# Adding two groups of output projections ahead of queued weights, and summing a norm's squares from folded halves

## The chip, the cores and the metric

One core of a Trainium2 chip runs the whole program in one launch. The metric is the device time in microseconds (us); lower is better.

## What is computed

Two transformer blocks over 256 tokens of width 1024, all in float32. The first block is causal attention and a convolutional feed-forward, with a norm at its end; the second is feed-forward, a mixer of two kinds of attention, and feed-forward again, each with a norm whose gain and shift come from a conditioning vector. Cut to the parts that matter here:

```
x = x + attention(rms_norm(x)) @ w_o            # phases qkv1, o1
x = x + conv_ffn(rms_norm(x))                   # phases up1, down1
x = rms_norm(x)
x = x + gate1 * swiglu(modulate(rms_norm(x)))   # phases up2, down2
x = x + gate2 * mixer(modulate(rms_norm(x)))    # phases qkv3, o3
x = x + gate3 * swiglu(modulate(rms_norm(x)))   # phases up4, down4

rms_norm(x) = x * rsqrt(mean(x * x, over the 1024 features) + eps) * gain
```

## The kernel before

The activations stay on the chip, transposed: `XT` holds 8 tiles of 128 features by 256 tokens. Each product in a phase takes its weights as slabs of 8 (or 6) row tiles by 256 columns. A slab is loaded by DMA into `raw` (3 buffers), ScalarE (ACT) rounds it by pairs of row tiles (a chunk, 128x512) into `whi`, VectorE (DVE) takes the rest into `wlo`, and TensorE (PE) multiplies each row tile in three matmuls: `whi` by the activation's high part, `whi` by its low part, `wlo` by the high part (L1353, L1356, L1357). Two tiles of output make a group; its last chunk lets VectorE take it out of PSUM (`evict`).

The order of the work on every engine is fixed by `Plan.lay` before the program is built. It writes one list of steps (`st.put`), and each engine walks through the list and issues its own part of each step, in order. `fill` puts a chunk's rounding (`hi`) and, one chunk later, its `lo`; `load` of slab i+3 follows the last `lo` of slab i. A semaphore stands between any two engines, and also between two instructions of one engine where the second reads what the first wrote.

The five norms (`qkv1`, `up1`, `up2`, `qkv3`, `up4`) get their sum of squares by pairs of tiles, q = 0 to 3: ScalarE squares pair 0 into `acc` and pairs 1 to 3 into `sq` (L769; L765 and L767 for the last pair of `up1`, tiles 6 and 7), and VectorE adds `sq` to `acc` (L992, 128x512: both halves at once). There is one `sq`, so the squares of pair q+1 wait for the add of pair q. Then TensorE multiplies `meanf` (1/1024 everywhere) with the halves of `acc` (L1374), which sums over the partitions; `up2` does this for two sums (j = 0, 1). ScalarE turns the result into `Rr` = rsqrt by an Ln and an Exp (L785, L788). In `up1` the last pair isn't added: TensorE sums it from `sq` directly (L1378). All phases but `up1` begin their products on the unnormed tiles (`B`, by L749 and L977) and need `Rr` only when their first groups are taken out; `qkv1` begins on `A` and scales at eviction; `up1` has to wait for `Rr`, makes y (L1011), its high part on ScalarE (L806) and its low part (L1018). While TensorE waits there it runs 9 idle matmuls (L1365).

`o1` and `o3` have their weights cut so that the last two row tiles of groups 0, 1 and 2 (slab `ot`, 6 steps of kt, in turn for the three groups) come after everything that these groups can do earlier; the last slab is group 3. The lines that order these evictions, the squares and the adds:

```
while tag == "ot" and kt % 2 == 1 and group - o_group <= kt - 3:
    ...
    evict(group)
```

So group 0 is taken out after kt = 3 of `ot`, groups 1 and 2 after kt = 5, behind the two chunks that `fill(pieces(tag, c0, kt))` has put there, and a step `sq` stands for both the squares (ScalarE) and their add (VectorE).

## Time and profile before

| | |
|---|---|
| median of 3 runs | 818.08 us (817.9 to 819.89) |
| profiled execution | 818.6 us, of which its span is 816.4 us |
| PE busy in the span | 800.4 us (98%) |
| DVE busy | 646.4 us (79%) |
| ACT busy | 487.2 us (60%) |
| granted TensorE clock | 1.00 of full speed, every stretch |

The span runs from the first to the last instruction that the hardware profiler recorded; the execution's own time has 2.2 us more around it. Busy times are sums over an engine's instructions; an engine can be busy and still not be the one that sets the end. In a timeline each line gives the start, the duration, the engine, the line of the kernel, the operation, output and input tiles and how many instructions were merged; in brackets stands how long the engine was idle just before, and who released it. A matmul of `meanf` is recorded twice (x4 for two), since float32 operands pass twice. Other matmuls overlap, so the distance between their starts is their price.

### The profile page before, as it was taken

To read this page: it belongs to the slowest core of one execution; us is meant where nothing else is said; L and a number is where in the kernel's file an instruction comes from. 1 tells how busy PE (TensorE), PEld (TensorE's weight loads), DVE (VectorE), ACT (ScalarE), POOL (GpSimd) and SP (SyncE) were. 2 spreads that over 40 slices of the span, in tenths; PEclk is the share of its full clock that TensorE was granted. 3 is DMA by queue.
4 is the path that set the end of the run, shared out by engine and by line. 5 is a ranking of instruction groups with operands and counts; after the bars stand their busy time and mean duration, and the time that the engine had idled before them with its cause. 6 is when DMAs were issued, how large, how long until landed. Compare 5 with 4: busy or idle time off the path is not lost.

```text
span 816.4 us, 16918 instructions
## 1 busy us (share of the span) xinstructions
PE 800.4 (98%) x6838; PEld 778.9 (95%) x6838; DVE 646.4 (79%) x1381; ACT 487.2 (60%) x1015; POOL 21.1 (3%) x53
## 2 busy tenths in 40 slices
PE   7999999999999999999999999899999999999998
PEld 7899998999999999999999999889889999999998
DVE  5788887889899887999988786977667896775551
ACT  6754565766766565755554556665755775555440
POOL 1000000000000000000000000700000000000000
PEclk9999999999999999999999999999999999999999
DMA  9776683765565988489998887545334578666640
GB/s 290 259 236 229 199 278 122 228 204 188 188 222 171 319 310 284 148 300 330 360 328 304 281 262 224 165 133 180 119 118 156 157 255 270 207 196 194 194 155 27
DMA packets 150013, 179.44 MB, mean 220 GB/s; under 512 B 5680, under 2 KB 139568, under 8 KB 149936
## 3 DMA queue, kind: packets, MB, share of 16 engines
q1 hardware_dynamic: 147680, 177.22, 66.1%
q8 instruction: 54, 0.88, 0.4%
q10 hardware_dynamic: 1232, 1.11, 0.4%
q0 software_dynamic: 1024, 0.03, 0.1%
q14 instruction: 23, 0.19, 0.1%
HBM read 177.27 MB, written 1.05 MB: 218 GB/s over the span
## 4 chain that ended last, share of the span: by engine, by line
PE 77%; DVE 4%; ACT 2%; issue 1%; DVEq 0%; ACTq 0%
PE bank L1353 25%; PE bank L1356 24%; PE bank L1357 24%; DVE wlo L971 1%; PE bank L1456 1%; PE bank L1444 1%; PE bank L1473 0%; PE bank L1374 0%; PE bank L1406 0%; DVE yb L1011 0%; PE bank L1423 0%; DVE A L1022 0%; ACT B L749 0%; PE bank L1399 0%; ACT sq L769 0%
## 5 line engine op out<-in xcount | busy, mean ns | idle before, releaser
L971 DVE TENSOR_TENSOR wlo<-raw,whi 128x512 fp32r<-128x512 f32 x528 | 343.2, 685 | 69.3 <-ACT whi L728 68.7
L728 ACT ACTIVATE whi<-raw 128x512 fp32r<-128x512 f32 x528 | 307.6, 622 | 96.6 <-PE bank L1357 86.0
L1353 PE MATMUL bank<-A,whi 128*128 128x256 f32 x1264 | 357.0, 282 | 2.9 <-DVE wlo L971 2.1
L1356 PE MATMUL bank<-A,whi 128*128 128x256 f32 x1264 | 350.0, 277 | 0.1
L1357 PE MATMUL bank<-A,wlo 128*128 128x256 f32 x1264 | 349.6, 277 | 0.0
L1353 PEld LDWEIGHTS bank<-A,whi 128*128 128x128 f32 x1264 | 237.6, 188 | 7.0 <-DVE wlo L971 3.0
L1356 PEld LDWEIGHTS bank<-A,whi 128*128 128x128 f32 x1264 | 237.5, 188 | 1.2 <-issue 1.0
L1357 PEld LDWEIGHTS bank<-A,wlo 128*128 128x128 f32 x1264 | 237.5, 188 | 0.0
L1353 PE MATMUL bank<-Hhi,whi 128*128 128x256 f32 x528 | 146.0, 276 | 0.0
L1357 PE MATMUL bank<-Hhi,wlo 128*128 128x256 f32 x528 | 145.7, 276 | 0.0
L1356 PE MATMUL bank<-Hlo,whi 128*128 128x256 f32 x528 | 145.7, 276 | 0.0
L1356 PEld LDWEIGHTS bank<-Hlo,whi 128*128 128x128 f32 x528 | 99.1, 188 | 0.0
L1353 PEld LDWEIGHTS bank<-Hhi,whi 128*128 128x128 f32 x528 | 99.1, 188 | 0.0
L1357 PEld LDWEIGHTS bank<-Hhi,wlo 128*128 128x128 f32 x528 | 99.1, 188 | 0.0
L1060 DVE SCALAR_TENSOR_TENSOR mring<-mring,cact 128x1024 f32<-128x1024 f32 x72 | 87.2, 1220 | 0.0
L1353 PE MATMUL bank<-B,whi 128*128 128x258 f32 (+1 forms) x184 | 52.8, 287 | 0.8 <-DVE B L977 0.8
L1356 PE MATMUL bank<-B,whi 128*128 128x258 f32 (+1 forms) x184 | 52.3, 284 | 0.0
L882 ACT ACTIVATE Hhi<-hb 128x256 fp32r<-128x256 f32 x33 | 13.8, 418 | 64.2 <-DVE hb L1153 38.6
L1357 PE MATMUL bank<-B,wlo 128*128 128x258 f32 (+1 forms) x184 | 51.8, 282 | 0.0
L1119 DVE SCALAR_TENSOR_TENSOR ca<-bank,cols,ca 128x255 f32<-128x255 f32 (+1 forms) x88 | 36.5, 476 | 2.0 <-ACT ca L848 1.8
L1353 PE MATMUL bank<-Ohi,whi 128*128 128x256 f32 x128 | 36.8, 288 | 0.0
L1357 PE MATMUL bank<-Ohi,wlo 128*128 128x256 f32 x128 | 35.6, 278 | 0.0
(150 smaller groups left out, 809.5 us busy)
## 6 DMA issues: line engine op xcount, KB each, us to landing
mring<-in_w_mod SPq DMA_DIRECT2D x72, 512.0 KB, 6.3
raw<-in_ffn_w_up SPq DMA_DIRECT2D x22, 1024.0 KB, 5.2
raw<-in_w_gate SPq DMA_DIRECT2D x22, 1024.0 KB, 5.8
raw<-in_w_up SPq DMA_DIRECT2D x22, 1024.0 KB, 5.5
raw<-in_w_down SPq DMA_DIRECT2D x16, 1024.0 KB, 5.8
raw<-in_w_in SPq DMA_DIRECT2D x12, 1024.0 KB, 5.6
raw<-in_moba_w_qkv SPq DMA_DIRECT2D x11, 1024.0 KB, 5.3
raw<-in_ffn_w_down SPq DMA_DIRECT2D x8, 1024.0 KB, 7.0
```

The source lines that it names most:

```text
L728: act.activation(whi[:, i % SPL, k0:k1, 0:width], raw[:, i % RAW, k0:k1, 0:width], ACT.Copy).then_inc(s_whi, 1)
L882: act.activation(Hhi[:, n, :], hb[:, 0, :], ACT.Copy).then_inc(s_hhi, 1)
L971: dve.tensor_tensor(lo, raw[:, i % RAW, k0:k1, 0:width], hi.bitcast(F32), ALU.subtract).then_inc(s_wlo, 1)
L1060: dve.scalar_tensor_tensor(out=w, in0=w, scalar=1.0, in1=cact[:, :], op0=ALU.mult, op1=ALU.mult, accum_out=msum[:, u:u + 1]).then_inc(s_ms ...
L1119: ins = dve.scalar_tensor_tensor(out=y[:, part:S], in0=at(g, i, 0, S - part), scalar=cvec[:, 2 - part, c:c + 1], in1=y[:, part:S], op0=ALU ...
L1353: pe.matmul(o, hi, xh, start=kg == 0 and not (j and halved(g)), stop=False)
L1356: pe.matmul(o, hi, xl, start=False, stop=False)
L1357: ins = pe.matmul(o, lo, xh, start=False, stop=final and (j == 1 or not halved(g)))
L1444: pe.matmul(b[:, 0:3 * P], upn[:, :], spl, start=True, stop=False)
L1456: ins = pe.matmul(o, Vn[:, t, (h + e) * 64:(h + e) * 64 + 64], w, start=t == 0, stop=t == 1)
```

## The change

- **Squares and adds are steps of their own** (`sq`, `add`). In `o1` and `o3`, groups 1 and 2 are both taken out directly after kt = 5 of `ot`, ahead of the two chunks; then come the squares of group 1, its add, and the squares of group 2. The add of group 2 moves into the last slab, after its kt = 3.
- **Folded halves.** The add of pair 2 is followed by an add of the two halves of `acc` into one (128x256), and pair 3 is added half by half to that one (two 128x256). TensorE then multiplies `meanf` with one half instead of two.
- **`up1`:** TensorE sums tile 6's squares as soon as they are there, then tile 7's.

```diff
...
             fill(1, force=True)
             lower()
-            st.put("sq", "qkv1", q)
-            st.put("sq", "qkv1", q + 1)
+            for k in (q, q + 1):
+                st.put("sq", "qkv1", k)
+                st.put("add", "qkv1", k)
         fill_through(1)
...
         norm = "qkv1"
         deferred = []
+
+        def taken(ph, c0):
+
+            to = NEXT_NORM[ph]
+            if ph == "o3" and c0 == 0:
+                st.put("modul", to)
+            if to != "up1":
+                for n in (c0 // P, c0 // P + 1):
+                    st.put("ain", to, n)
+            st.put("sq", to, c0 // C)
 
...
                         st.put("out", n)
                 else:
-                    to = NEXT_NORM[ph]
-                    if ph == "o3" and c0 == 0:
-                        st.put("modul", to)
-                    if to != "up1":
-                        for n in (c0 // P, c0 // P + 1):
-                            st.put("ain", to, n)
-                    st.put("sq", to, c0 // C)
+                    taken(ph, c0)
+                    st.put("add", NEXT_NORM[ph], c0 // C)
 
...
                     done += 1
                     self.chunk_done[i, kt // 2] = done
+                    if tag == "ot" and kt == 5:
+                        both = (group, group + 1)
+                        for k in both:
+                            self.group_end[k] = done
+                            self.groups.append((ph, "o", (k - o_group) * C))
+                            st.put("evict", k, 0)
+                        taken(ph, C)
+                        st.put("add", NEXT_NORM[ph], 1)
+                        taken(ph, 2 * C)
+                        group += 2
+                    if tag == "o" and c0 == 3 * C and kt == 3:
+                        st.put("add", NEXT_NORM[ph], 2)
                     offer(i + SPL, kt + 1)
...
                     for _ in range(MOD_STEPS[ph](i)):
                         mod_step()
-                while tag == "ot" and kt % 2 == 1 and group - o_group <= kt - 3:
+                if tag == "ot" and kt == 3:
                     self.group_end[group] = done
...
-        s_sq, s_acc, s_sums, s_ln, s_root = sem("s_sq"), sem("s_acc"), sem("s_sums"), sem("s_ln"), sem("s_root")
+        s_sq6, s_fold, s_sq, s_acc, s_sums, s_ln, s_root = sem("s_sq6"), sem("s_fold"), sem("s_sq"), sem("s_acc"), sem("s_sums"), sem("s_ln"), sem("s_root")
...
+        fold_index = {part: k + 1 for k, part in enumerate(p for p in acc_index if p[1] > 1)}
...
                         o = sq[:, :, :]
                     if ph == "up1" and q == 3:
-                        act.activation(o[:, 0, :], XT[:, 6, :], ACT.Square)
+                        act.activation(o[:, 0, :], XT[:, 6, :], ACT.Square).then_inc(s_sq6, 1)
                         x_here(ph, 7)
...
                     need.wait_ge(s_sq, sq_index[ph, q, j])
                     need.wait_ge(s_acc, acc_index[ph, q, j] - 1)
-                    dve.tensor_tensor(acc[:, j, :, :], acc[:, j, :, :], sq[:, :, :], ALU.add).then_inc(s_acc, 1)
+                    one, two = acc[:, j, 0, :], acc[:, j, 1, :]
+                    if q == 1:
+                        dve.tensor_tensor(acc[:, j, :, :], acc[:, j, :, :], sq[:, :, :], ALU.add).then_inc(s_acc, 1)
+                    elif q == 2:
+                        dve.tensor_tensor(acc[:, j, :, :], acc[:, j, :, :], sq[:, :, :], ALU.add).then_inc(s_fold, 1)
+                        need.wait_ge(s_fold, fold_index[ph, q, j])
+                        dve.tensor_tensor(one, one, two, ALU.add).then_inc(s_acc, 1)
+                    else:
+                        dve.tensor_tensor(one, one, sq[:, 0, :], ALU.add).then_inc(s_fold, 1)
+                        need.wait_ge(s_fold, fold_index[ph, q, j])
+                        dve.tensor_tensor(one, one, sq[:, 1, :], ALU.add).then_inc(s_acc, 1)
 
...
-            part_of = {"lo": weights, "ain": a_in, "sq": add_squares, "latey": late_y, "latelo": late_lo, "modul": modulate,
+            part_of = {"lo": weights, "ain": a_in, "add": add_squares, "latey": late_y, "latelo": late_lo, "modul": modulate,
...
                 for j in range(2 if ph == "up2" else 1):
                     need.wait_ge(s_acc, acc_index[ph, 2 if late else 3, j])
-                    for t in range(2):
-                        ins = pe.matmul(b[:, j * S:(j + 1) * S], meanf[:, :], acc[:, j, t, :], start=t == 0, stop=t == 1 and not late)
+                    ins = pe.matmul(b[:, j * S:(j + 1) * S], meanf[:, :], acc[:, j, 0, :], start=True, stop=not late)
                 if late:
+                    need.wait_ge(s_sq6, 1)
+                    pe.matmul(b[:, 0:S], meanf[:, :], sq[:, 0, :], start=False, stop=False)
                     need.wait_ge(s_sq, sq_index[ph, 3, 0])
-                    for t in range(2):
-                        ins = pe.matmul(b[:, 0:S], meanf[:, :], sq[:, t, :], start=False, stop=t == 1)
+                    ins = pe.matmul(b[:, 0:S], meanf[:, :], sq[:, 1, :], start=False, stop=True)
                 ins.then_inc(s_sums, 1)
...
```

In the rows below, taken from the program's order, each line is one step of an engine, with the line of its own kernel and the semaphores it waits for in brackets.

VectorE at the start, around `qkv1`'s norm; `acc<-acc,sq` are the adds. Before:

```order
L971 TENSOR_TENSOR wlo<-raw,whi 128x512 [waits s_whi]
L992 TENSOR_TENSOR acc<-acc,sq 128x512 [waits s_sq]
L971 TENSOR_TENSOR wlo<-raw,whi 128x512 [waits s_whi]
L992 TENSOR_TENSOR acc<-acc,sq 128x512 [waits s_acc,s_sq] x2
L971 TENSOR_TENSOR wlo<-raw,whi 128x512 [waits s_whi] x3
L1087 SCALAR_TENSOR_TENSOR QKV<-bank,Rr 128x256 [waits s_root,s_chunk]
```

Changed:

```order
L990 TENSOR_TENSOR wlo<-raw,whi 128x512 [waits s_whi]
L1013 TENSOR_TENSOR acc<-acc,sq 128x512 [waits s_sq]
L990 TENSOR_TENSOR wlo<-raw,whi 128x512 [waits s_whi]
L1015 TENSOR_TENSOR acc<-acc,sq 128x512 [waits s_acc,s_sq]
L1017 TENSOR_TENSOR acc<-acc 128x256 [waits s_fold]
L1019 TENSOR_TENSOR acc<-acc,sq 128x256 [waits s_acc,s_sq]
L1021 TENSOR_TENSOR acc<-acc,sq 128x256 [waits s_fold]
L990 TENSOR_TENSOR wlo<-raw,whi 128x512 [waits s_whi] x3
L1116 SCALAR_TENSOR_TENSOR QKV<-bank,Rr 128x256 [waits s_root,s_chunk]
```

Behind the third add there is a fold, and the fourth is in two parts, each waiting for the one ahead.

VectorE at the end of `o1`; `XT<-bank,XT` is a tile's eviction, two to a group, `wlo<-raw,whi` a chunk's low part. Before:

```order
L1202 TENSOR_TENSOR XT<-bank,XT 128x256 [waits s_alo]
L971 TENSOR_TENSOR wlo<-raw,whi 128x512 [waits s_whi] x2
L1202 TENSOR_TENSOR XT<-bank,XT 128x256 [waits s_alo,s_x1,s_chunk]
L1202 TENSOR_TENSOR XT<-bank,XT 128x256 [waits s_alo]
L992 TENSOR_TENSOR acc<-acc,sq 128x512 [waits s_sq]
L1202 TENSOR_TENSOR XT<-bank,XT 128x256 [waits s_alo,s_x2]
L1202 TENSOR_TENSOR XT<-bank,XT 128x256 [waits s_alo]
L992 TENSOR_TENSOR acc<-acc,sq 128x512 [waits s_acc,s_sq]
L971 TENSOR_TENSOR wlo<-raw,whi 128x512 [waits s_whi] x2
L1202 TENSOR_TENSOR XT<-bank,XT 128x256 [waits s_alo,s_x3,s_chunk]
L1202 TENSOR_TENSOR XT<-bank,XT 128x256 [waits s_alo]
```

Changed:

```order
L1231 TENSOR_TENSOR XT<-bank,XT 128x256 [waits s_alo]
L1231 TENSOR_TENSOR XT<-bank,XT 128x256 [waits s_alo,s_x1,s_chunk]
L1231 TENSOR_TENSOR XT<-bank,XT 128x256 [waits s_alo]
L1231 TENSOR_TENSOR XT<-bank,XT 128x256 [waits s_alo,s_x2]
L1231 TENSOR_TENSOR XT<-bank,XT 128x256 [waits s_alo]
L1013 TENSOR_TENSOR acc<-acc,sq 128x512 [waits s_sq]
L990 TENSOR_TENSOR wlo<-raw,whi 128x512 [waits s_whi] x3
L1015 TENSOR_TENSOR acc<-acc,sq 128x512 [waits s_acc,s_sq]
L1017 TENSOR_TENSOR acc<-acc 128x256 [waits s_fold]
L990 TENSOR_TENSOR wlo<-raw,whi 128x512 [waits s_whi]
L1231 TENSOR_TENSOR XT<-bank,XT 128x256 [waits s_alo,s_x3,s_chunk]
L1231 TENSOR_TENSOR XT<-bank,XT 128x256 [waits s_alo]
```

The evictions of groups 1 and 2 stand together ahead of all weights, and one add with its fold stands behind three chunks of weights, ahead of group 3's eviction. In `o3` the order changes in the same way, with the tiles' low parts of `B` between.

ScalarE at the same place; `sq<-XT` are squares, `whi<-raw` the chunks' roundings. Before:

```order
L769 ACTIVATE acc<-XT 128x512 [waits s_evicted,s_xeven]
L728 ACTIVATE whi<-raw 128x512 [waits s_chunk]
L728 ACTIVATE whi<-raw 128x512
L769 ACTIVATE sq<-XT 128x512 [waits s_acc,s_evicted,s_xeven] x2
L728 ACTIVATE whi<-raw 128x512 [waits s_chunk,s_raw0]
L728 ACTIVATE whi<-raw 128x512 [waits s_chunk]
L765 ACTIVATE sq<-XT 128x256 [waits s_acc,s_xeven]
L767 ACTIVATE sq<-XT 128x256 [waits s_evicted]
```

Changed:

```order
L788 ACTIVATE acc<-XT 128x512 [waits s_evicted,s_xeven]
L788 ACTIVATE sq<-XT 128x512 [waits s_acc,s_evicted,s_xeven] x2
L747 ACTIVATE whi<-raw 128x512 [waits s_chunk]
L747 ACTIVATE whi<-raw 128x512
L747 ACTIVATE whi<-raw 128x512 [waits s_chunk,s_raw0]
L747 ACTIVATE whi<-raw 128x512 [waits s_chunk]
L784 ACTIVATE sq<-XT 128x256 [waits s_acc,s_xeven]
L786 ACTIVATE sq<-XT 128x256 [waits s_evicted]
```

Two roundings that stood ahead of the squares of groups 1 and 2 now stand behind them.

## Rows read from the trace of the kernel before

**Rows 1.** The page's head and its busy times.

```profile
span 816.4 us, 16918 instructions
...
PE 800.4 (98%) x6838; PEld 778.9 (95%) x6838; DVE 646.4 (79%) x1381; ACT 487.2 (60%) x1015; POOL 21.1 (3%) x53
```

**Rows 2.** Waits of TensorE (PE): us in total, times, longest us.

```profile
PE bank L1467 <- DVE QKV L1105: 1.5, 1, 1.5
PE bank L1378 <- ACT sq L767: 1.2, 1, 1.2
PE bank L1374 <- DVE acc L992: 1.1, 2, 0.6
```

**Rows 3.** Timeline, TensorE around `up2`'s norm: start us, us, then the instruction.

```profile
321.27 0.28 PE L1357 MATMUL bank<-B,wlo 128*128 128x258 f32 x1
321.38 1.89 PE L1374 MATMUL bank<-acc,meanf 128*128 128x256 f32 x8
322.92 0.47 PE L1353 MATMUL bank<-B,whi 128*128 128x258 f32 x1
323.23 0.29 PE L1356 MATMUL bank<-B,whi 128*128 128x258 f32 x1
```

**Rows 4.** Timeline, all engines, around `qkv1`'s norm.

```profile
16.69 0.69 DVE L992 TENSOR_TENSOR acc<-acc,sq 128x512 f32<-128x512 f32 x1
...
17.42 0.63 ACT L769 ACTIVATE sq<-XT 128x512 f32<-128x512 f32 x1 [0.76 <-DVE acc L992]
...
17.95 2.18 ACT L728 ACTIVATE whi<-raw 128x512 fp32r<-128x512 f32 x4
...
18.08 0.69 DVE L992 TENSOR_TENSOR acc<-acc,sq 128x512 f32<-128x512 f32 x1 [0.70 <-ACT sq L769]
...
18.92 1.10 PE L1374 MATMUL bank<-acc,meanf 128*128 128x256 f32 x4 [0.63 <-DVE acc L992]
...
20.12 0.48 ACT L785 ACTIVATE lnb<-bank,epsc 128x256 f32<-128x256 f32 x1
```

**Rows 5.** Timeline, behind that norm: ScalarE, then TensorE.

```profile
22.70 0.30 ACT L779 ACTIVATE fcol<-fcol,epsc 128x8 f32<-128x8 f32 x1 [1.13 <-DVE fcol L984]
...
32.68 0.55 PE L1423 MATMUL bank<-identf,W 128*128 128x128 f32 x3 [0.70 <-DVE W L1266]
```

**Rows 6.** Timeline, all engines, from `o1` to `up1`.

```profile
122.74 0.75 DVE L1202 TENSOR_TENSOR XT<-bank,XT 128x256 f32<-128x256 f32 x2
...
126.21 0.28 PE L1356 MATMUL bank<-Olo,whi 128*128 128x256 f32 x1
...
126.33 0.28 PE L1357 MATMUL bank<-Ohi,wlo 128*128 128x256 f32 x1
126.34 0.69 DVE L992 TENSOR_TENSOR acc<-acc,sq 128x512 f32<-128x512 f32 x1 [0.75 <-ACT sq L769]
126.95 1.29 DVE L971 TENSOR_TENSOR wlo<-raw,whi 128x512 fp32r<-128x512 f32 x2
...
128.15 0.75 DVE L1202 TENSOR_TENSOR XT<-bank,XT 128x256 f32<-128x256 f32 x2
...
129.40 1.13 PE L1378 MATMUL bank<-sq,meanf 128*128 128x256 f32 x4 [1.19 <-ACT sq L767]
```

**Rows 7.** Timeline, VectorE behind `qkv3`'s norm.

```profile
504.07 0.43 DVE L1221 TENSOR_TENSOR tmp<-bank,Rr 8x256 f32<-8x256 f32 x1 [0.50 <-ACT Rr L788]
...
504.54 0.43 DVE L1224 TENSOR_SCALAR tmp<-tmp,bank,cols 8x256 f32<-8x256 f32 x1
```

**Rows 8.** Timeline, from `o3` to `up4`.

```profile
624.76 1.33 DVE L971 TENSOR_TENSOR wlo<-raw,whi 128x512 fp32r<-128x512 f32 x2
...
628.85 0.28 PE L1353 MATMUL bank<-B,whi 128*128 128x258 f32 x1
...
632.39 0.87 DVE L1204 SCALAR_TENSOR_TENSOR XT<-bank,hcol,XT 128x256 f32<-128x256 f32 x2
...
634.08 0.36 PE L1353 MATMUL bank<-B,whi 128*128 128x258 f32 x1 [0.76 <-DVE B L977]
```

## The prediction

> **What bounds the kernel now.** I read the page's head first: TensorE is busy for 800.4 of 816.4 us, VectorE for 646.4 [rows 1]. So a matmul taken away is worth its own time wherever TensorE runs without gaps, and work moved between VectorE and ScalarE is worth something only where TensorE waits for it. The waits of TensorE say where that is [rows 2]: the two waits for `acc` (one at `qkv1`'s norm, one at the end of `o1`), one of 1.2 us for the squares of tile 7, and one of 1.5 us for VectorE in `qkv3`. Then I read the timelines around each norm and each place that the order changes. "Slower", "faster" and "the same" below mean by more or less than 0.3%, 2.45 us, about what a measurement of this kernel can tell from no change.
>
> **The price of a mean matmul.** In `up2` four of them (8 passes) stand between two starts that are 323.23 - 321.27 = 1.96 us apart [rows 3]. Two ordinary distances of 0.12 belong to the neighbours, so a pass costs 1.72 / 8 = 0.215 and a matmul 0.43 us. Around it TensorE doesn't stop, so in `up2` the two that go are worth **-0.86**. The squares' chain of `up2` gets longer by two folds and two splits, which end before the norm's matmuls are reached, beside products of a slab.
>
> **The price of a fold.** A 128x256 operation on VectorE takes about 0.42, for two independent ones 0.75 together [rows 6], so the second adds 0.33. Where the second waits for the first by a semaphore, it starts after the first's end: 504.07 + 0.43, then 504.54 [rows 7], a handover of 0.04. A fold behind an add is therefore 0.46, and an add in two parts is 0.42 + 0.04 + 0.42 = 0.88 in place of 0.69, which is +0.19. In all six folds and five splits make VectorE's work 6 x 0.46 + 5 x 0.19 = 3.7 us longer.
> The Trainium skill ("VectorE: DVE Perf Modes", The DRAIN you can't avoid) says that the semaphore itself costs nothing, since the next operation waits for the pipeline to empty with or without it. The rows speak against that for these shapes, since the independent one starts 0.09 before the other's end. By the page the start, below, would lose about 0.1 less, and the sum would be -3.0.
>
> **Start, `qkv1`.** The add of pair 2 ends at 16.69 + 0.69 = 17.38, the squares of pair 3 start at 17.42 for that reason, the last add at 18.08, TensorE's norm at 18.92 after 0.63 of waiting [rows 4]. The fold stands between the first two, since `sq` is free only when it is done: +0.46. The split adds 0.19, so TensorE's norm comes 0.65 later; it saves 0.43 by one matmul less; left +0.22. But another chain runs on: the four roundings behind the squares (17.95, 2.18 long) and Ln (20.12), which follows without a gap [rows 4], all shift by 0.46, and with them `Rr`, the first eviction, VectorE's `fcol` behind it, and ScalarE, which waits 1.13 for `fcol` and is then busy without a pause up to the attention's first weights, for which TensorE waits 0.70 at 32.68 [rows 5]. There the longer chain counts. I take **+0.46**; the ends are +0.22 (if it finds slack) and +0.65 (if the matmul is not won back).
>
> **From `o1` to `up1`.** Here TensorE is stopped from its last product (126.33 + 0.28 = 126.61) to the squares of tile 7 at 129.40, but for `acc`. Group 3 could be taken out at about 126.65 and is at 128.15, since VectorE first waited 0.75 for group 2's squares, then added them (126.34) and did two chunks of weights (126.95) [rows 6]. Changed: the last slab is 48 matmuls of 0.12 back from 126.33, so groups 1 and 2 are finished at about 121.0, not 122.7. Their four evictions end at 121.0 + 3 x 0.33 + 0.42 = 122.4, group 1's squares (0.63, as in rows 4) at 122.4 too, its add at 123.15, group 2's squares at 123.8. Then two roundings and their `lo` take turns, the third `lo` ends at 125.65, the add runs to 126.3, the fold to 126.7, the last `lo` to 127.3 with 0.08 of overlap; group 3 goes out at 127.2, 0.93 earlier. Behind it tile 6 is summed while tile 7 is squared, so one matmul of 0.43 is left behind tile 7 where two were. `up1` begins with y, A and the products in the same distances as now. **-1.34**, between -0.43 (VectorE's queue is as late as before) and -1.93 (group 3 goes out when TensorE is done). The `wlo` that move back are for `up1`'s first slab, which starts only once `Rr` is there; its next load is issued when the third `lo` is done, which is earlier than now, so SP's queue isn't held.
>
> **`qkv3`.** One matmul less is -0.43, but VectorE had idled only 0.50 before `Rr` [rows 7] and comes 0.19 later by the split; so `Rr` finds it free 0.31 earlier, and behind it VectorE is full until TensorE waits 1.5 us for it [rows 2]. **-0.31**, between -0.43 and -0.12.
>
> **From `o3` to `up4`.** One matmul less, TensorE without gaps: **-0.43**. Before that, TensorE waits 0.76 at 634.08 for tile 6's B, which hangs on group 3's eviction at 632.39 [rows 8]. Changed, VectorE starts four evictions at 624.76, where two `lo` were, and has ahead of group 3: 4 evictions and 4 low parts at 0.38 each, the four `lo` at 0.60, an add of 0.61, an add of 0.69 and a fold of 0.42. That is 3.0 + 2.4 + 1.7 = 7.2 us, and 632.0. I take **-0.38**, half the wait, between 0 and -0.76, since ScalarE's turns between can hold it.
>
> **Sum.** 0.46 - 1.34 - 0.86 - 0.31 - 0.43 - 0.38 = -2.86. Against the profiled execution's own 818.6 us that is 815.7; the median of the runs shown, 818.08, lies 0.5 below it, so the forecast is **815.2 us**. The folds elsewhere (`down1`, `down2`) I cost at nothing: ScalarE rounds ahead there until TensorE frees a buffer, and a slab of products covers them; without that cover they'd cost their 0.46 each.
>
> **Rivals.**
> 1. *The boundaries give little.* ScalarE's new order (squares ahead of roundings) holds the third and fourth `lo`, so group 3 goes out no earlier at either boundary. Then only matmuls are won: 0.46 - 0.43 - 0.86 - 0.31 - 0.43 = -1.57, 816.5. For it: VectorE's gain in `o3` hangs on three hand-overs with ScalarE. Against: in `o1` it stood idle twice for 0.75, which goes.
> 2. *The boundaries give all.* The waits go whole and the start finds slack: 0.22 - 1.93 - 0.86 - 0.43 - 0.43 - 0.76 = -4.19, 813.9.
> 3. *Each VectorE instruction counts.* All 3.7 us of added work shows, because VectorE is 79% busy. The matmuls on the path give 5 x 0.43 + 0.43 = 2.6, the earlier eviction 1.3: -3.9 + 3.7 = -0.2, 817.9. Against it: VectorE is idle for 170 us of the span [rows 1], and most adds stand where TensorE has products in hand. The Trainium skill's page named above (Rules for kernel authors) advises to keep the count of chained operations small; that rule speaks against this change.
> 4. *Slower.* In `o3` the weights' `lo` for the second chunk of `up4` stand behind two evictions, four low parts and an add that waits for ScalarE. TensorE starts `up4` at 628.85 [rows 8] and wants that chunk 12 matmuls of 0.12 later, 630.3; I have it at 629.2 to 629.5. Each us by which it is late beyond about 1 us is a us of TensorE. It turns the sum to no change at 3.9 us of lateness, and to slower by 0.3% at 6.3 us, 820.5. Against it: nothing in that chain is longer than an instruction.
> That the change doesn't do what it says is hardly possible: its order shows one `meanf` matmul where there were two.
>
> **Chances.** The forecast's case 0.52, of which a tenth may miss the 0.3% since it lies only 0.4 us beyond it; rival 1 0.23, rival 2 0.11, rival 3 0.08, rival 4 0.06. Faster: 0.47 + 0.11 = 0.58; the same: 0.05 + 0.23 + 0.08 = 0.36; slower 0.06. The range reaches from rival 2 with some spread of runs, 813.4, past rival 1 to rival 3's edge, 817.8.
>
> **What would show it.** Right: TensorE's `acc` matmul at the start about 0.65 later and the wait at 32.68 longer; `up2`'s four passes in place of eight; at the end of `o1` group 3 out 1 us after the last product's start, and `up1`'s first product some 0.9 us earlier relative to the last product of `o1`, 0.4 more by the sum's shorter tail; the wait for tile 6's B about halved. Wrong: a new wait of TensorE for `wlo` at the start of `up4`, the wait of 1.5 us in `qkv3` grown by more than 0.3, or a wait before a norm other than `qkv1`'s.

## The result, and the profile after

The changed kernel takes 815.77 us in the median of 7 runs (815.51 to 817.14), the kernel before 818.02 in 7 runs beside them. The ratio is 0.9968, 95% interval 0.9958 to 0.9978, so the change is clear of zero. The medians lie 2.25 us apart, which is 0.28%; the ratio, which isn't the quotient of the medians, says 0.32%. Two of the seven runs, the profiled one among them, took 1.4 to 1.5 us longer than the middle of the other five and had a mean granted clock of 0.997, where the others had 0.999 or 1.0; they are called the longer kind below. A second set on another occasion (label `e0_whole`, below) gave 815.48 against 818.04, ratio 0.9967 (0.9955 to 0.998). The forecast was 815.2, in a range from 813.4 to 817.8.

The page of the changed kernel's profiled execution, which itself took 817.14 us. It answers to [rows 1].

```profile
span 814.9 us, 16905 instructions
...
PE 799.3 (98%) x6826; PEld 777.8 (95%) x6826; DVE 649.6 (80%) x1392; ACT 487.7 (60%) x1015; POOL 21.1 (3%) x53
```

VectorE has 11 instructions more, as counted, and is busy 3.2 us longer (3.7 forecast; 2.5 in the second set's profile, 648.9). TensorE has 12 recorded passes fewer, and yet is busy only 1.1 us less, where 12 x 0.215 = 2.6 went. In the second set's profile it is busy for 797.8 us, which is the whole 2.6 less. The missing 1.5 us of the first profile are the surprise of this case and have their own part below.

The waits of TensorE, changed kernel, to hold against [rows 2]:

```profile
PE bank L1496 <- DVE QKV L1134: 1.6, 1, 1.6
PE bank L1402 <- DVE acc L1021: 1.3, 1, 1.3
...
PE bank L1382 <- DVE QKV L1134: 1.0, 1, 1.0
...
PE bank L1405 <- ACT sq L784: 0.7, 1, 0.7
PE bank L1402 <- DVE acc L1017: 0.5, 1, 0.5
```

The wait for tile 7's squares (1.2 us before) is now one for tile 6's, of 0.7. The wait at `qkv1`'s norm has doubled from 0.63 to 1.3, as the longer chain of adds lets one expect; what of that reaches the end is less, as shown below. Of the two in `qkv3`, both for VectorE's evictions, the larger is 1.6 (1.5 before).

To find where the time went I cut the span at points of TensorE that both kernels have: the first product after 10.2 us, the third of the four V transposes of `qkv1` (84 us), and further on the first reset (a `meanf` matmul of one column) of `up1` and the second of `up2`, the first and the last V transposes of `qkv3`, the second reset of `up4`, and the end. In us, from the profiled executions (start of the later mark less start of the earlier):

| stretch, at the times of before | before | changed | changed, second set | forecast, difference |
|---|---|---|---|---|
| 10.6 to 84.2, the start | 73.57 | 73.96 | 73.79 | +0.46 |
| 84.2 to 138.7, `o1` to `up1` | 54.55 | 53.41 | 53.43 | -1.34 |
| 138.7 to 339.0, `up2`'s norm | 200.26 | 199.40 | 199.40 | -0.86 |
| 339.0 to 525.5, `qkv3` | 186.49 | 186.22 | 186.19 | -0.31 |
| 525.5 to 603.0, rest of the attention | 77.54 | 79.10 | 77.41 | 0 |
| 603.0 to 654.1, `o3` to `up4` | 51.02 | 50.17 | 50.17 | -0.81 |
| 654.1 to 816.4, the end | 162.30 | 162.30 | 162.29 | 0 |

Five stretches moved as forecast in sign and nearly in size. The first row is the roughest, since its first mark wanders: over the kernels that ran without `qkv1`'s fold it lies between 73.33 and 73.77. The fifth row is 1.56 longer in one execution and not in the other of the same kernel, so that is no effect of the order.

Timeline of the changed kernel at `qkv1`'s norm, all engines, against [rows 4] and the first of [rows 5]:

```profile
16.44 0.69 DVE L1015 TENSOR_TENSOR acc<-acc,sq 128x512 f32<-128x512 f32 x1
17.17 0.42 DVE L1017 TENSOR_TENSOR acc<-acc 128x256 f32<-128x256 f32 x1
17.63 0.63 ACT L788 ACTIVATE sq<-XT 128x512 f32<-128x512 f32 x1 [1.22 <-DVE acc L1017]
18.16 2.17 ACT L747 ACTIVATE whi<-raw 128x512 fp32r<-128x512 f32 x4
18.29 0.42 DVE L1019 TENSOR_TENSOR acc<-acc,sq 128x256 f32<-128x256 f32 x1 [0.70 <-ACT sq L788]
18.75 0.42 DVE L1021 TENSOR_TENSOR acc<-acc,sq 128x256 f32<-128x256 f32 x1
...
19.32 0.67 PE L1402 MATMUL bank<-acc,meanf 128*128 128x256 f32 x2 [1.29 <-DVE acc L1021]
20.25 0.46 ACT L804 ACTIVATE lnb<-bank,epsc 128x256 f32<-128x256 f32 x1
...
32.79 0.55 PE L1452 MATMUL bank<-identf,W 128*128 128x128 f32 x3 [0.75 <-DVE W L1295]
```

From the start of pair 2's add the squares are 1.19 away (0.73 before), the norm's matmul 2.88 (2.23 before: +0.65, as forecast), but Ln 3.81 (3.43 before), and the transposes of the first attention weights 16.35 (15.99 before). So the start costs 0.36. The V transposes at 84 us still show it: 67.87 behind that add (84.31 - 16.44), 67.50 before.

From `o1` to `up1`, against [rows 6]:

```profile
121.07 1.42 DVE L1231 TENSOR_TENSOR XT<-bank,XT 128x256 f32<-128x256 f32 x4 [0.60 <-PE bank L1386]
121.91 0.63 ACT L788 ACTIVATE sq<-XT 128x512 f32<-128x512 f32 x1 [0.71 <-DVE XT L1231]
...
123.38 0.63 ACT L788 ACTIVATE sq<-XT 128x512 f32<-128x512 f32 x1 [0.84 <-DVE acc L1013]
123.92 2.18 ACT L747 ACTIVATE whi<-raw 128x512 fp32r<-128x512 f32 x4
124.57 1.29 DVE L990 TENSOR_TENSOR wlo<-raw,whi 128x512 fp32r<-128x512 f32 x2 [0.70 <-ACT whi L747]
125.78 0.68 DVE L1015 TENSOR_TENSOR acc<-acc,sq 128x512 f32<-128x512 f32 x1
126.50 0.43 DVE L1017 TENSOR_TENSOR acc<-acc 128x256 f32<-128x256 f32 x1
126.84 0.69 DVE L990 TENSOR_TENSOR wlo<-raw,whi 128x512 fp32r<-128x512 f32 x1
...
127.44 0.75 DVE L1231 TENSOR_TENSOR XT<-bank,XT 128x256 f32<-128x256 f32 x2
...
128.36 0.70 PE L1405 MATMUL bank<-sq,meanf 128*128 128x256 f32 x2 [0.69 <-ACT sq L784]
128.90 0.59 PE L1407 MATMUL bank<-sq,meanf 128*128 128x256 f32 x2
```

The evictions of groups 1 and 2 stand together, and the second add starts without a wait, where VectorE had waited 0.75 for the squares; a wait of 0.70 for ScalarE's roundings has come in ahead of two `lo`. Group 3 is taken out at 127.44, which is 43.13 behind the mark at 84.31; before it was 128.15 - 84.19 = 43.96. So it goes out 0.83 earlier (0.93 forecast); it is then 1.25 behind the start of the last product, at 126.19, where 1 us was forecast. The stretch from the end of tile 7's squares to Ln lasts 0.89 in place of 1.22: -0.33 for the tail (-0.43 forecast).

`up2`'s norm, TensorE, against [rows 3]:

```profile
320.25 0.28 PE L1386 MATMUL bank<-B,wlo 128*128 128x258 f32 x1
320.37 1.03 PE L1402 MATMUL bank<-acc,meanf 128*128 128x256 f32 x4
321.04 0.47 PE L1382 MATMUL bank<-B,whi 128*128 128x258 f32 x1
321.35 0.29 PE L1385 MATMUL bank<-B,whi 128*128 128x258 f32 x1
```

Half the passes, and between the same neighbours 321.35 - 320.25 = 1.10 where 1.96 were: 0.86 less, as in the stretch.

From `o3` to `up4`, VectorE and then TensorE, against [rows 8]:

```profile
631.40 0.87 DVE L1233 SCALAR_TENSOR_TENSOR XT<-bank,hcol,XT 128x256 f32<-128x256 f32 x2
...
632.71 0.29 PE L1386 MATMUL bank<-B,wlo 128*128 128x258 f32 x1
633.09 0.36 PE L1382 MATMUL bank<-B,whi 128*128 128x258 f32 x1
```

This execution passed the mark at 603 us 0.59 earlier than before's, so group 3 goes out at 631.99 on before's scale, against 632.39; I had worked out 632.0. The matmul that waits for tile 6's `B` starts 30.65 behind the mark (633.09 - 602.44), and 31.05 before (634.08 - 603.03). So its wait is down by 0.40, as much as the eviction moved. (The distance to its predecessor, 0.38 here, is no measure of that, since some records of matmuls are missing: the profile of the variant without `qkv1`'s fold has the same place at 30.65 with an idle time of 0.36 in front.) Nothing waits for the weights of `up4`'s second chunk.

### The profile page after: what moved, and what is told of

It is laid out like the page before. It is cut to its first block, busy times and chain, and to the rows that moved or that the text cites. A ratio compares the mean times of both kernels' runs of the same rounds, so it can differ in the third digit from the quotient of the medians.

```text
span 814.9 us, 16905 instructions
## 1 busy us (share of the span) xinstructions
PE 799.3 (98%) x6826; PEld 777.8 (95%) x6826; DVE 649.6 (80%) x1392; ACT 487.7 (60%) x1015; POOL 21.1 (3%) x53
## 3 DMA queue, kind: packets, MB, share of 16 engines
HBM read 177.27 MB, written 1.05 MB: 219 GB/s over the span
## 4 chain that ended last, share of the span: by engine, by line
PE 87%; DVE 5%; ACT 5%; DMA 1%; issue 1%; SPq 0%; DVEq 0%; ACTq 0%
PE bank L1382 27%; PE bank L1385 27%; PE bank L1386 27%; DVE wlo L990 2%; PE bank L1485 1%; DMA raw<-in_moba_w_qkv 1%; ACT whi L747 1%; PE bank L1435 1%; PE bank L1452 1%; PE bank L1473 1%; ACT W L934 1%; ACT W L935 1%; PE bank L1496 0%; PE bank L1502 0%; DVE yb L1040 0%
```

## The experiments

Each took one part, or put one thing in; the diffs are against the changed kernel where nothing else is said. Ratios are to the kernel before, on the same chip in the same set of runs. There were three sets on three chips, and in them the kernel before had medians of 818.10, 818.04 and 818.36; so runs of different sets are compared by their distance from it.

**Only the folded halves** (the order and `up1`'s tail as before: the new lines of the plan and the `s_sq6` matmul taken out):

```diff
-                    if tag == "ot" and kt == 5:
-                        both = (group, group + 1)
...
-                if tag == "ot" and kt == 3:
+                while tag == "ot" and kt % 2 == 1 and group - o_group <= kt - 3:
```

> Only the folded halves (squares and evictions in the old order, tile 6 and 7 summed together). Theory A (each term stands for itself, worth what it does to TensorE's path): start +0.4, `up2` -0.86, `qkv3` -0.3, `up4` -0.43, and at the ends of `o1` and `o3` the fold now stands ahead of group 3's eviction without the new order to pay for it, +0.4 each: -0.4 us in all, no change that can be told. Theory B (a mean matmul is worth its 0.43 wherever it goes and VectorE's folds are covered): 5 x 0.43 less, -2.1 us. Theory C (all of VectorE's 3.7 us of added work shows): +1.5 us.

Measured: 817.68 us (11 runs, 817.4 to 818.87), ratio 0.9995 (0.9986 to 1.0004). By stretch: `up2` -0.86, `qkv3` -0.27, `o3` to `up4` 0.00 (51.02). The last is two things that cancel: a matmul less, and tile 6's `B` later by the fold. The wait for it is 1.22 where [rows 8] had 0.76:

```profile
634.83 0.36 PE L1370 MATMUL bank<-B,whi 128*128 128x258 f32 x1 [1.22 <-DVE B L984]
```

In `o1` the fold stands ahead of group 3's eviction too, which is 44.35 behind the 84 us mark (43.96 before): +0.39. Folds alone are worth about nothing: what TensorE saves in `up2`, `qkv3` and `up4`, VectorE's queue loses at the start and ahead of group 3 in `o1` and in `o3`. The medians lie 0.42 apart, where the theory of small terms had 0.4; but no change is inside the interval too. The two rivals, -2.1 and +1.5, are outside it. The stretch from `o1` to `up1` can't be used here: 55.67, since the clock fell in it in this profile (last part).

**Only the new order** (all adds and matmuls of the norms as before):

```diff
-                    if q == 1:
+                    if q == 1 or True:
...
-                    ins = pe.matmul(b[:, j * S:(j + 1) * S], meanf[:, :], acc[:, j, 0, :], start=True, stop=not late)
+                    n_half = 2 if True else 1
+                    for t in range(n_half):
+                        ins = pe.matmul(b[:, j * S:(j + 1) * S], meanf[:, :], acc[:, j, t, :], start=t == 0, stop=t == n_half - 1 and not late)
```

> Only the new order at the ends of `o1` and `o3` (both halves of `acc` summed by TensorE as before, tile 6 and 7 together). Theory A: group 3 goes out about 1.3 us earlier in `o1`, since no fold stands ahead of it, and the wait of 0.76 for tile 6's B in `o3` goes nearly whole: -2.0 us in all. Theory B (the gain of the whole is the matmuls'): -0.5 us or less.

Measured: 816.32 us (11 runs, 816.05 to 816.73), ratio 0.9977 (0.9968 to 0.9985). `o1` to `up1` is 53.14 (-1.41), `o3` to `up4` 50.13 (-0.89): group 3 goes out 42.54 behind the mark, 1.42 earlier than before, and the wait for tile 6's `B` is gone. The medians lie 1.78 apart (-2.0 expected, -0.5 by the rival). So the order does most of the work, and it does more of it without the folds. It also shows what the fold in `up4` is worth: 50.13 without it, 50.17 with it. There the matmul of 0.43 less is paid back by group 3 going out 0.46 later (28.50 behind the mark at 603 us here, 28.96 in the whole change).

**Only tile 6 ahead of tile 7** (against the kernel before):

```diff
-                    for t in range(2):
-                        ins = pe.matmul(b[:, 0:S], meanf[:, :], sq[:, t, :], start=False, stop=t == 1)
+                    need.wait_ge(s_sq6, 1)
+                    pe.matmul(b[:, 0:S], meanf[:, :], sq[:, 0, :], start=False, stop=False)
...
+                    ins = pe.matmul(b[:, 0:S], meanf[:, :], sq[:, 1, :], start=False, stop=True)
```

> Only tile 6's squares summed ahead of tile 7's. Theory A: one matmul of 0.43 moves out of the tail, -0.4 us, and nothing else changes. Rival: the second of the two starts anew after a wait, as dear as a first one, -0.2 us. Both are below what the timed runs can tell, so the timeline around `up1`'s norm decides: distance from the end of tile 7's squares to Ln 1.22 before, 0.8 by A, 1.0 by the rival.

Measured: 817.99 us (11 runs, 817.3 to 819.5), ratio 0.9999 (0.999 to 1.0008). The total can't resolve it; the stretch from `o1` to `up1` can: 54.19, -0.36. Ln waits 0.89 for TensorE, as in the whole change.

```profile
130.04 0.47 ACT L792 ACTIVATE lnb<-bank,epsc 128x256 f32<-128x256 f32 x1 [0.89 <-PE bank L1397]
```

Before it waited 1.22. That is between the 0.8 of the theory and the 1.0 of the rival, and neither had the reason. Taking the matmul of tile 6 out of the tail was worth 0.33 to 0.36, not 0.43. In the whole change the squares of tile 7 end at 128.23 + 0.42 = 128.65 and TensorE begins on them at 128.90, 0.25 later, since tile 6's product holds it; before it began 0.05 behind them (129.40 [rows 6], squares to 129.35). The product for tile 6 takes more behind a wait than on a busy TensorE: from its start to the next one's it is 128.90 - 128.36 = 0.54. So 0.54 left the tail and 0.2 of it came back as a wait behind tile 6, which makes 0.34.

**The whole change without `qkv1`'s fold:**

```diff
-        fold_index = {part: k + 1 for k, part in enumerate(p for p in acc_index if p[1] > 1)}
+        fold_index = {part: k + 1 for k, part in enumerate(p for p in acc_index if p[1] > 1 and p[0] not in ('qkv1',))}
...
-                    if q == 1:
+                    if q == 1 or ph in ('qkv1',):
```

> The whole change, but `qkv1` keeps both halves (no fold, no split there). Theory A (the start's longer chain costs 0.3 to 0.46 net of its matmul): 0.4 us below the whole change, -3.0 from before; the wait before `qkv1`'s norm back at about 0.6 and the one behind it, before the first transposes, at 0.70. Rival (the start has slack and only the matmul counts): 0.43 above... no gain, so as the whole change or up to 0.2 slower.

Measured: 815.34 us (6 runs, 815.24 to 815.54), ratio 0.9967 (0.9955 to 0.9979). From pair 2's add to the transposes at 32.6 us it is 15.99, the value of before. The medians lie 2.76 below the kernel before, the whole change's 2.25 and 2.56 in its two sets; that agrees with a gain of 0.36 but doesn't measure it.

**The changed kernel again**, as the control of the next runs:

> The changed kernel again, beside its own variants on one chip, so that they can be compared with it and not only with the kernel before. Expected 815.6 to 815.9, 2.2 to 2.5 below the kernel before. If the 1.5 us by which some of its executions are longer belong to the granted clock behind the stall in qkv3, some runs here read 817.0 to 817.3 with a mean clock of 0.997 or 0.998, the rest 815.3 to 815.9 with 1.0.

Measured: 815.48 us (5 runs, 815.29 to 815.65), ratio 0.9967 (0.9955 to 0.998). None of the five was of the longer kind.

**Without the folds of `qkv1` and `up1`:**

```diff
+        fold_index = {part: k + 1 for k, part in enumerate(p for p in acc_index if p[1] > 1 and p[0] not in ('qkv1', 'up1'))}
...
+                    if q == 1 or ph in ('qkv1', 'up1'):
...
+                    n_half = 2 if ph in ('qkv1', 'up1') else 1
```

> The changed kernel without the fold in qkv1 and in up1; the other norms fold as before. My account: in up1 the fold of 0.46 stands on VectorE ahead of the last weights' low part and group 3's eviction, which sets the end of o1, so without it group 3 goes out about 0.4 earlier, and the two extra passes of the acc matmul run while TensorE waits anyway: the segment 84 to 138.7 us is 52.8 to 53.0 against 53.4. With the start's 0.4 the total is 814.8 to 815.0, against 815.7 for the whole change and 815.3 with only the start's fold taken out. Rival (the eviction waits for ScalarE or for TensorE's last product, not for VectorE): segment 53.3 to 53.8, total 815.3 or more.

Measured: **814.67 us** (5 runs, 814.62 to 814.81), ratio 0.9958 (0.9945 to 0.997). The stretch is 52.90, -1.65. VectorE and TensorE at the end of `o1`, where this execution's mark is at 84.06:

```profile
125.50 0.68 DVE L1013 TENSOR_TENSOR acc<-acc,sq 128x512 f32<-128x512 f32 x1
...
126.25 1.12 PE L1404 MATMUL bank<-acc,meanf 128*128 128x256 f32 x4
126.71 0.75 DVE L1231 TENSOR_TENSOR XT<-bank,XT 128x256 f32<-128x256 f32 x2
```

Group 3 goes out 42.65 behind the mark, 0.48 earlier than with the fold, about the 0.46 of a fold, and nothing is lost, since the two extra passes of the `acc` matmul lie in a time in which TensorE waits for group 3 anyway. This is the best version of all that ran, 0.8 us below the whole change on the same chip.

**One more dependent operation behind `qkv1`'s fold:**

```diff
-                        dve.tensor_tensor(one, one, two, ALU.add).then_inc(s_acc, 1)
+                        if ph == "qkv1":
+                            dve.tensor_tensor(one, one, two, ALU.add).then_inc(s_more, 1)
+                            need.wait_ge(s_more, 1)
+                            dve.tensor_tensor(one, one, one, ALU.max).then_inc(s_acc, 1)
+                        else:
+                            dve.tensor_tensor(one, one, two, ALU.add).then_inc(s_acc, 1)
```

> The changed kernel, with one more dependent 128x256 operation of VectorE behind qkv1's fold (the maximum of the half with itself, which changes no value). Measured from the start of the add of pair 2, the whole change moved TensorE's wait at 32.7 us by 0.36 (15.99 without the fold, 16.35 with it), where the fold itself moved the squares by 0.45. My account: 0.09 was slack, as the rounded weights of ScalarE ended 0.1 before Ln could start on TensorE's sum; that slack is used up, so the further operation costs its whole 0.46, distance 16.81. Rival (each costs 0.36, as something behind absorbs a part of any delay): 16.71. Rival (VectorE's next work hides it): under 16.5.

Measured, in one execution (815.57 us): the transposes start at 33.07, the add at 16.26, which makes 16.81, as expected.

```profile
16.26 0.69 DVE L1015 TENSOR_TENSOR acc<-acc,sq 128x512 f32<-128x512 f32 x1
16.99 0.42 DVE L1018 TENSOR_TENSOR acc<-acc 128x256 f32<-128x256 f32 x1
17.45 0.43 DVE L1020 TENSOR_TENSOR acc<-acc 128x256 f32<-128x256 f32 x1
17.91 0.63 ACT L788 ACTIVATE sq<-XT 128x512 f32<-128x512 f32 x1 [1.68 <-DVE acc L1020]
```

So a dependent 128x256 operation costs 0.46, and the first one cost 0.36 only because 0.1 of slack lay behind it. Dependent ones start 17.45 - 16.99 = 0.46 apart; of two evictions of the same shape that don't depend on each other (L1231 x2, 0.75 for both) the second adds 0.33. The evictions read PSUM, so that pair is not quite the same operation, but at 128x512 with all operands in SBUF it is alike: the fold starts 17.17 - 16.44 = 0.73 behind its add in the changed kernel, and the second of two independent `lo` adds 1.29 - 0.69 = 0.60. In both, a dependence costs 0.13. The Trainium skill ("VectorE: DVE Perf Modes", The DRAIN you can't avoid) measured copies, with and without semaphores, and has the semaphore cost nothing. The rows don't agree with that as a general rule; the same section does say that some next operations start earlier, without a figure.

**Late steps of `qkv3` at every third row tile.** This was meant to take away TensorE's waits of 1.0 and 1.6 us:

```diff
-                if ready and not deferred and kt % 2 == 0 and (i > self.first_of[ph] + 1 or kt > 3):
+                if ready and not deferred and (((i - self.first_of[ph]) * 8 + kt) % 3 if ph == "qkv3" else kt % 2) == 0 and (i > self.first_of[ph] + 1 or kt > 3):
```

> The changed kernel, with the late y and lo steps of qkv3 offered at every third row tile instead of every second, so that VectorE has fewer of them per slab in the first slabs. Theory A (VectorE's work behind Rr is the bound of qkv3's first slabs, and the two waits of 0.96 and 1.60 us come from it): both shrink and the segment from 339 to 525.5 us gets 1.5 to 2.5 us shorter, 813.3 to 814.3 in all. Rival (the same work has to be done before the same transposes, wherever it stands): the waits move to the later y steps, time unchanged within 0.5 us.

Measured: 818.61 us (11 runs, 817.23 to 818.86), ratio 0.9998 (0.9989 to 1.0007): 3.1 above the changed kernel in the medians. A miss, for neither theory. Up to the V transposes it does gain 1.05 (185.14), since the first wait goes; then a new one of 2.41 us stands at 529 us. ScalarE and VectorE there, with TensorE's wait:

```profile
522.66 0.51 ACT L828 ACTIVATE A<-yb,modT 128x256 fp32r<-128x256 f32 x1 [1.56 <-DVE yb L1040]
...
527.58 1.14 ACT L747 ACTIVATE whi<-raw 128x512 fp32r<-128x512 f32 x2
...
528.24 0.69 DVE L990 TENSOR_TENSOR wlo<-raw,whi 128x512 fp32r<-128x512 f32 x1 [1.59 <-ACT whi L747]
528.85 0.55 DVE L1302 SCALAR_TENSOR_TENSOR W<-bank,W 128x384 f32<-128x384 f32 x1
...
529.45 1.01 PE L1473 MATMUL bank<-W,upn 128*128 128x384 f32 x2 [2.41 <-DVE W L1302]
```

VectorE stands idle for 1.59 us with the attention's weights `W` next in its queue but one, because the `lo` ahead of them waits for a rounding of ScalarE. That `lo` stands ahead of `W` in the changed kernel too; what is new is that the rounding is late, 5.29 us behind the V transposes (527.58 - 522.29) where it was 2.39. The rows show why. ScalarE works without a pause from 522.66 to this rounding, and before 522.66 it had waited 1.56 for a late y (`yb`), which VectorE now makes at 522.15, behind the four operations that make `QKV`; in the changed kernel's second profile it made it at 518.81, ahead of them. A step was moved, and what it was moved behind was not counted. This is read from the two timelines; no run took the late y back.

The eleven runs fall in two heaps: five from 817.23 to 817.5, six from 818.61 to 818.86 (four of five of the first with a mean clock of 1.0, five of the six others 0.998). So of the 3.1 us about 1.8 belong to the new order of steps, and the rest to what sets the heaps apart. This led to the next three.

**The same, with TensorE kept busy in the wait of 2.41 us:**

```diff
+                t_free("later", n)
+                if heads[n][1] == "qkv3" and not kept:
+                    kept.append(n)
+                    for _ in range(8):
+                        pe.matmul(b[:, 0:P], meanf[:, :], meanf[:, :], start=True, stop=True)
                 need.wait_ge(s_sp, stick[n])
-                t_free("later", n)
```

> The kernel of e6_space, with eight matmuls of meanf by meanf issued ahead of TensorE's wait of 2.41 us in it (measured in e5_keep: six took 1.50 us, so eight take about 2.0), into the bank that the waiting matmul overwrites. Theory A: e6_space lost 1.4 us in 6 of its 11 runs to a lower granted clock, because TensorE had idled there for 2.41 us. With the idle time filled no run does, all read 817.2 to 817.6 with a mean clock of 0.999 or 1.0, and the stretch behind the wait is at the clock 1.00 in the profile. Rival (the clock falls for another reason, such as what the other engines do in those microseconds): again about half the runs read 818.6 to 818.9 with a clock of 0.998.

Measured: 817.41 us (11 runs, 817.25 to 818.05), ratio 0.999 (0.9981 to 1.0). The heap at 818.6 and above is gone: 0 of 11 runs, where 6 of 11 were in it. The two ran in different sets on different chips, and the unfilled one was not repeated beside the filled one. In the profile TensorE now idles 0.70 there and works in the rest of the wait. The stretches of 2 us behind the wait, without and with the filling; the column after the engines is the granted clock:

```profile
528.00:530.00 2.00, 0.55 (x2) 0.42 (x3) 1.73 (x4) 0.72 (x2) 0.31 (x1) 1.00 1.00 366
530.00:532.00 2.00, 2.00 (x10) 1.42 (x10) 2.00 (x5) 1.32 (x3) 0.00 (x0) 0.53 1.09 353
532.00:534.00 2.00, 2.00 (x16) 1.71 (x13) 1.34 (x3) 1.37 (x4) 0.00 (x0) 0.61 0.03 10
```

```profile
528.00:530.00 2.00, 2.00 (x18) 1.87 (x17) 1.81 (x4) 0.64 (x2) 0.21 (x1) 1.00 1.02 378
530.00:532.00 2.00, 2.00 (x18) 1.57 (x17) 2.00 (x5) 1.40 (x3) 0.00 (x0) 1.00 1.05 340
```

VectorE and ScalarE do nearly the same work at the same places in both; what differs most is what TensorE did before. The expectation's narrower part failed: four runs lie above 817.6, up to 818.05, and three show a mean clock of 0.998. So some loss is left elsewhere, and I did not find where.

**The changed kernel, with six such matmuls ahead of its wait of 1.6 us:**

```diff
-                emptied(need, qkv_group[ph, tile])
...
+                if ph == "qkv3" and not kept:
+                    kept.append(1)
+                    for _ in range(6):
+                        pe.matmul(b[:, 0:P], meanf[:, :], meanf[:, :], start=True, stop=True)
+                emptied(need, qkv_group[ph, tile])
```

> The changed kernel, with six matmuls of meanf by meanf (about 0.12 us each, into the bank that the transposes overwrite behind them) issued in qkv3 just before TensorE's long wait for VectorE at 523 us. Theory A: the clock fell in after's profile since TensorE had idled 0.96 and then 1.60 us there; with the idle time filled to under 1 us no run shows the lower clock there, and the time is that of the changed kernel's undisturbed runs, 815.3 to 815.9, as TensorE waits for VectorE anyway. Rival: the clock's falls have nothing to do with this stall, then about 2 runs in 11 still read 1.5 us more with a clock of 0.997 or 0.998.

Measured: 815.46 us (7 runs, 815.12 to 816.46), ratio 0.9971 (0.996 to 0.9982). No run has a clock under 0.999, but the control had none either in its 5, so this doesn't tell the theories apart: 2 longer runs in 12 without the filling, 0 in 7 with it, is what chance gives often. Two runs at 816.25 and 816.46 with a clock of 1.0 are a spread that I can't explain; so not every longer run comes with a lower clock.

**Both: without two folds, with the filling in `qkv3`:**

> The version that should be the best of those tried: the changed kernel without the fold in qkv1 and up1 (e7_up1), with the six filling matmuls ahead of the wait in qkv3 (e5_keep). My account: 814.6 to 814.8 as e7_up1, and no run with a clock under 0.999; the filling matmuls cost nothing since TensorE waits there for VectorE. Rival: they hold the transposes or disturb the next slab, 815.0 or more.

Measured: 815.01 us (5 runs, 814.67 to 815.42), ratio 0.9962 (0.995 to 0.9975). That is 0.3 above the version without the filling (814.67), but on another chip, where the kernel before is 0.3 slower as well: 3.35 below it here, 3.37 there. So the filling neither gained nor cost anything that can be told, and the rival's 815.0 isn't borne out either. The filling isn't worth having here; leaving the two folds out is.

## Why the prediction was right, point by point

- **Start.** Forecast +0.46, measured +0.36, inside the stated ends. The step "Ln follows without a gap" read a coincidence as a bound: before, Ln at 20.12 followed both the fourth rounding (end 20.13) and TensorE's sum (18.92 + 1.10 = 20.02), and an instruction that needs nothing from its predecessor can start a little before that one's end, as Ln now does, by 0.08 (20.25 against 18.16 + 2.17 = 20.33). So the bound before was the sum, and ScalarE's queue had 0.1 of slack. The further operation, which found no slack, cost the whole 0.46.
- **`o1` to `up1`.** Forecast -1.34, measured -1.13. Group 3's eviction 0.83 earlier instead of 0.93, and the tail 0.33 instead of 0.43 (these two forecasts make 1.36, not the 1.34 that was added up). The tail's term was the matmul's price on a busy TensorE, taken over to a place where it waits, and it left out that tile 7's product would have to wait for tile 6's. That the fold stands in that chain was in the working but not drawn out as a choice: order alone gave -1.41 there, order and tail without the fold -1.65.
- **`up2`.** -0.86 forecast and measured, to the last digit: TensorE has no gap there, so the price of a pass could be read from the distance of two starts.
- **`qkv3`.** -0.31 forecast, -0.27 and -0.30 measured.
- **`o3` to `up4`.** -0.81 forecast, -0.85 measured; the eviction's time of 632.0, counted up instruction by instruction, was met. "Half the wait" was a choice, 0.38, and the wait went down by 0.40. What the forecast didn't see is that the fold itself takes the other half: without it the wait goes whole, and the two terms of this place, the matmul and the fold ahead of group 3, cancel (50.13 and 50.17).
- **The folds elsewhere** (`down1`, `down2`) cost nothing, as said: the stretches with `down1` and with `down2` in them moved by no more than their norms' terms.
- **The sum.** The terms as measured give 0.36 - 1.13 - 0.86 - 0.28 - 0.85 = -2.76 against -2.86. The medians differ by 2.25 in the one set and 2.56 in the other; the two longer runs in seven make 0.15 of that difference, and the ends of the intervals cover the rest. That the sum came out within 0.1 is in part luck: the start was put 0.10 too dear and `o1` to `up1` 0.21 too good. And the word "faster", by the 0.3% that the prediction set, is not settled: the ratio's 0.32% has an interval on both sides of it, and the medians give 0.28 and 0.31%.
- **The rivals.** 1 (boundaries give little) lost at 816.5: both evictions came earlier. 2 (all) was nearly reached in `o3` by the order alone, where the wait went whole, and not with the folds. 3 (each VectorE instruction counts) is wrong as a rule, since `up2`'s and `qkv3`'s folds cost nothing or little beside what they save, and right in three places where VectorE's chain sets the end: in `qkv1` and `up1`, where the fold costs more than the matmul gives, and in `up4`, where it costs the same. The Trainium skill's advice ("VectorE: DVE Perf Modes", Rules for kernel authors) to keep the number of chained operations small holds for `qkv1` and `up1`: leaving their folds out gained 0.8 us. 4 (late weights in `up4`) didn't occur.

## What to carry to other kernels

Price a trade between two engines place by place: the same edit (one TensorE matmul less for 0.46 us more of VectorE) gained 0.43 where TensorE ran without gaps, came out even in `up4`, where the fold stood ahead of an eviction that TensorE waits for, and lost 0.36 to 0.5 where TensorE stood waiting for VectorE at the norm or for group 3 anyway. The best version that ran makes it in three norms of five; by the rows two of them, `up2` and `qkv3`, would do, which didn't run. When a step in a single ordered list is moved, read off what now stands ahead of the next step that someone waits for; the attempt that looked only at the steps it spread out lost 1.8 us in its shorter runs and 3.1 in the median. And where an instruction follows another without a gap, check by a second row whether it also has another releaser that ended just then, before calling the first its bound.

## What the runs showed of the hardware that I had not expected

In the changed kernel's profiled execution TensorE's clock fell to its lower level, 1.2 GHz, between 523 and 528 us. The stretches around the wait in `qkv3` (after the engines: granted clock, DMA share, GB/s):

```profile
523.00:524.00 1.00, 0.66 (x5) 0.67 (x6) 1.00 (x4) 0.97 (x3) 1.00 (x3) 0.93 0.96 256
524.00:527.00 3.00, 3.00 (x16) 3.00 (x16) 2.86 (x6) 2.79 (x6) 3.00 (x8) 0.50 0.98 271
```

The second profile of the same kernel, at the same place:

```profile
524.00:527.00 3.00, 3.00 (x29) 3.00 (x28) 2.85 (x5) 2.87 (x6) 3.00 (x8) 1.00 1.00 285
```

And two of TensorE's matmuls behind the fall, in the first profile:

```profile
524.43 0.41 PE L1382 MATMUL bank<-A,whi 128*128 128x256 f32 x1
524.65 0.41 PE L1385 MATMUL bank<-A,whi 128*128 128x256 f32 x1
```

Their starts are 0.22 apart, where 0.115 is usual; in the 3 us from 524 there are 16 records of matmuls, and 29 in the second profile, where the clock stayed. TensorE is busy all through the stretch in both, so 13 matmuls of 0.115, 1.5 us, are what the fall costs, and the fifth stretch of the table is 1.56 longer. Before the fall TensorE had idled 0.96 and then 1.60 us within 7 us. The Trainium skill ("TensorE: Matmul & The Clock Gate", Part 1: The HAM clock gate (the "warmup" mystery)) knows two levels only, half and full; the rows agree, with 0.50 inside the stretch and a value between, 0.93, in a slice that holds an edge.

It is not decided by the program alone, nor by these two waits: in its second profile the same kernel idled 0.94 and 1.60 us at the same places and kept the clock at 1.00. Runs of the longer kind, by 1.2 to 1.5 us, were 2 of 12 of the changed kernel and 3 of 11 with the folds only, in whose profile the clock fell behind the end of `o1`, after waits of 1.17 and 1.62 us. The kernel before had such runs too, 3 of 17 in the second set (819.17 to 819.32, mean clock 0.998), so the change didn't bring them in. They were 6 of 11 where the wait was 2.41 us, and 0 of 11 when that wait was filled. That speaks for an idle TensorE as the cause in this last case, though the two were on different chips; three of the 11 filled runs still show a mean clock of 0.998. For the wait of 1.6 us it is argued from one profile, the second one speaks against these waits being enough, and the test there didn't decide. For a comparison of kernels that differ by 2 us it means that a single profiled execution may carry 1.5 us of this, and that one looks at the granted clock by stretches before explaining a difference.
